# Two transformer layers written out one behind the other in every engine's program, in place of a loop over them

## What is computed

```python
def second_block(x, positions, ...):
    for l in range(DEPTH_2):                      # DEPTH_2 = 2
        mix = token_mixers(x, positions, lam_init, w_in[l], ...)   # four kinds of attention, gated
        x = layer_norm(DN_ALPHA * x + mix, ln1_g[l], ln1_b[l])
        ffn = grouped_moe(x, w_router, router_bias, moe_w1[l], moe_w3[l], moe_w2[l])  # 32 experts
        x = layer_norm(DN_ALPHA * x + ffn, ln2_g[l], ln2_b[l])
    return x
```

## Time and profile before

| | us |
|---|---|
| median of 3 runs (2465.21 to 2465.91) | 2465.53 |
| span of the profiled execution | 2463.8 |
| straight part, up to the layers | about 1055 |
| first pass of the loop, L2751 at 1055.20 to L2751 at 1756.89 | 701.69 |
| second pass, from L2751 at 1756.89 to the end at 2463.8 | 706.9 |

### The profile page before, as it was taken

How to read it: one execution, slowest core, us unless ns; L and a number is a source line. 1 busy time by engine, 2 the same in 40 slices (tenths; PEclk the granted TensorE clock), 3 DMA queues, 4 the chain that set the end, 5 groups by cost and what they waited for, 6 DMA issues and landing times.

```text
span 2463.8 us, 25868 instructions
## 1 busy us (share of the span) xinstructions
PE 2283.6 (93%) x10168; PEld 1569.8 (64%) x10168; DVE 831.3 (34%) x1478; ACT 490.2 (20%) x904; POOL 37.1 (2%) x82
## 2 busy tenths in 40 slices
PE   6999999999988899999999799999799998799997
PEld 3677778756866599768887443334478885533333
DVE  3332332544632365522225411122313144411213
ACT  2111222331312144412221111000102220200101
POOL 0000000100000000000000000000000000000000
PEclk8999999999997999999999899999899999899999
DMA  9555431311310345453212178877533121578792
GB/s 373 213 205 205 171 126 57 117 69 69 137 69 1 137 165 195 151 204 137 103 69 86 45 311 343 336 304 310 202 141 132 69 82 51 209 306 337 323 385 94
DMA packets 49273, 433.46 MB, mean 176 GB/s; under 512 B 6656, under 2 KB 7936, under 8 KB 16000
## 3 DMA queue, kind: packets, MB, share of 16 engines
q1 hardware_dynamic: 45296, 423.35, 44.1%
q10 hardware_dynamic: 3856, 8.42, 1.0%
HBM read 430.71 MB, written 1.05 MB: 175 GB/s over the span
## 4 chain that ended last, share of the span: by engine, by line
issue 57%; PE 39%; DVE 2%; ACT 1%; DMA 1%; POOL 1%; DVEq 0%; POOLq 0%; SPq 0%; ACTq 0%
PE bank L2428 15%; PE bank L2421 5%; PE bank L3062 5%; PE bank L3064 2%; PE bank L3115 2%; PE bank L2365 1%; PE bank L3117 1%; PE bank L2572 1%; PE bank L2530 1%; DMA ring<-in_early 1%; PE bank L3130 1%; PE bank L3026 1%; PE bank L2542 1%; PE bank L2552 1%; PE bank L2377 0%
## 5 line engine op out<-in xcount | busy, mean ns | idle before, releaser
L2421 PE MATMUL bank<-HT,ring 128*128 128x256 f32 (+1 forms) x1984 | 466.6, 395 | 8.1 <-issue 5.9
L2421 PEld LDWEIGHTS bank<-HT,ring 128*128 128x128 f32 x1984 | 375.1, 191 | 91.7 <-issue 45.2
L2428 PE MATMUL bank<-HT_HI,W_HI 128*128 128x512 f32 (+1 forms) x704 | 239.3, 340 | 8.3 <-DVE ring_lo L1564 4.1
L2428 PE MATMUL bank<-HT_HI,ring_lo 128*128 128x512 f32 (+1 forms) x704 | 240.1, 341 | 0.0
L2428 PE MATMUL bank<-HT_LO,W_HI 128*128 128x512 f32 (+1 forms) x704 | 238.1, 338 | 0.0
L3062 PE MATMUL bank<-ring,TOKENS 128*128 128x512 f32 x416 | 190.2, 600 | 3.7 <-issue 3.7
L1012 ACT ACTIVATE W_HI<-ring 128x2048 fp32r<-128x2048 f32 x66 | 126.4, 1915 | 294.6 <-PE bank L2428 228.4
L1564 DVE TENSOR_TENSOR ring_lo<-ring,W_HI 128x2048 fp32r<-128x2048 f32 x66 | 151.0, 2288 | 52.9 <-ACT W_HI L1012 52.8
L2324 DVE SCALAR_TENSOR_TENSOR tmp<-th,bank 128x256 f32<-128x256 f32 x50 | 21.1, 421 | 413.7 <-ACT th L1356 413.7
L2428 PEld LDWEIGHTS bank<-HT_HI,W_HI 128*128 128x128 f32 x704 | 133.3, 189 | 36.2 <-issue 17.1
L2428 PEld LDWEIGHTS bank<-HT_HI,ring_lo 128*128 128x128 f32 x704 | 134.6, 191 | 14.6
(11 more groups left out here) (473 smaller groups left out, 2794.8 us busy)
## 6 DMA issues: line engine op xcount, KB each, us to landing
ring<-in_early SPq DMA_DIRECT2D x64, 2048.0 KB, 8.4
ring<-in_l_moe_in SPq DMA_DIRECT2D x38, 2048.0 KB, 12.3
ring<-in_l_dense SPq DMA_DIRECT2D x30, 2048.0 KB, 7.8
ring<-in_l_moe_out SPq DMA_DIRECT2D x12, 2048.0 KB, 11.6
slot<-in_l_moe_in SPq DMA_DIRECT2D x10, 2048.0 KB, 8.5
HT<-in_l_moe_in SPq DMA_DIRECT2D x8, 2048.0 KB, 10.6
slot_xg<-in_l_moe_in SPq DMA_DIRECT2D x8, 2048.0 KB, 10.9
ring<-in_l_moe_out SPq DMA_DIRECT2D x14, 1024.0 KB, 11.3
```

Of the source, the lines that this page charges most:

```text
L2421: last = mm(out, w[:, k0 + k, c0:c0 + P], rhs(k), start=k == 0, stop=k == kn - 1)
L2428: last = mm(out, a, b, start=start and n == 0, stop=stop and n == 2)
```

## The change

In all five programs `with <engine>.Fori(0, LAYERS) as L:` becomes `for L in range(LAYERS):`, a loop of the language in which the program is written. The body is written out twice, once with `L = 0` and once with `L = 1`; every value made from `L` is a constant; and there is no counter and no branch back. The order of the work on every engine stays the same, and so do its matmuls, transfers and semaphores.

```diff
@@ block.sync @@
-            with sp.Fori(0, LAYERS) as L:
+            for L in range(LAYERS):
                 def free_slot(u):
                     sp.wait_ge(slot_free[u % 4], L * LAYER_TURNS + layer_turn(u))
@@ block.scalar @@
-            with se.Fori(0, LAYERS) as L:
+            for L in range(LAYERS):
 
                 se.wait_ge(layer_start, L + 1)
@@ block.gpsimd @@
-            with po.Fori(0, LAYERS) as L:
+            for L in range(LAYERS):
                 po.wait_ge(c_squares_ready, L + 1)
@@ block.vector @@
-            with ve.Fori(0, LAYERS) as L:
+            for L in range(LAYERS):
                 ve.drain().then_inc(layer_start, 1)
@@ block.tensor @@
-            with pe.Fori(0, LAYERS) as L:
+            for L in range(LAYERS):
                 def take(job):
                     return acquire(pe, at(L, job))
```

## The result

| | median (range), us | ratio to the kernel before, 95% interval |
|---|---|---|
| before | 2465.72 (2465.21 to 2467.15) | |
| after | 2452.51 (2445.63 to 2453.65) | 0.9938 [0.9924, 0.9953] |

So the change saves 13.2 us, 0.6%. The profiled execution took 2452.81 us with a span of 2451.0, 12.8 less than the earlier trace rows. First the page, the span and the busy time of each engine.

What follows compares the result with a forecast made beforehand. The prediction took PE as the bound, busy 2283.6 of 2463.8 us. Branch 4.0, registers 8.0, DVE and ACT 0.3 and clock 2.4 sum to 14.7, giving span 2449.1 and 2450.8 timed, range 2444.5 to 2459.5.

Steps and rivals of the forecast that it cites:

- Part 1: Between the layers on PE: without the taken branch and three steps around it, the second L2751 starts 4.0 us earlier.
- Part 2: In PE's short issue gaps: 91 exposed register steps of 0.09 us go, taken as 8.0 us, bounds 0 and 14.4.
- The list of lines: PE's short gaps: L3094, L2888, L3130 fall to 0.11 or 0.15 us, mostly leaving the issue rows; L3062 keeps its 0.2.
- DVE and ACT: Their adds matter only where PE waits, in the router and at layer end: 0.3 us for both layers, bounds 0 and 1.
- Part 3: Second L2751: with less idle time ahead, PE's half-speed clock there mostly goes, gaining 2.4 us, bounds 0 and 2.7.
- case E: The branch goes, but the low clock stays or moves to other matmuls: 2453.2, up to 2455.5; inside the forecast's 0.72.
- plus or minus 2 us, taken as nothing: Other low-clock stretches, at layer norms and router, may fall on more or fewer matmuls; counted as zero in the sum.
- The first layer: The first pass, which has no branch in it, gets shorter by about 4 us, separating Part 1 from Part 2.
- A: Rival: only the branch counts, as the adds hide in PE's drains; 2459.1 us, chance 0.11.
- D: Rival: waits are still worked out or a barrier comes in, so nothing changes; 2465.5 us, chance 0.04.
- C: Rival: fetching written-out code stalls PE's sequencer, 3.76 us a stall; 2469.6 with five, 2534 at worst; chance 0.04.
- B: Rival: all steps in PE's gaps go (14.4 us), and DVE's and ACT's too, 22.1 us together; 2443.4 us, chance 0.09.

Runs made afterwards that it cites:

- e1b: Kernel before with both layers written out on all engines, but the layer number kept in a register, so register instructions stay and no branch is taken back; 2455.48 us, 0.9970.
- e2: Kernel before with the two layers written out in PE's program alone, the other four engines keeping their loops; 2449.05 us, 0.9938.
- e5: Kernel after with PE's two waits at L2920 named in the other order, ACT's late copy first and the free bank second; 2452.25 us, 0.9953.
- e3: Kernel after with PE's loop kept, so only SP, ACT, POOL and DVE are written out; 2469.62 us, 1.0018 against the kernel before.
- e10: Kernel after with e7's edits, the wait order also swapped on ACT and DVE, and PE's next-weights wait moved ahead of the releasing drain; 2447.15 us, 0.9928.
- a1: Kernel after run again unchanged; 2451.29 us, 0.9948.
- e6: Kernel after with PE's waits in the experts moved ahead of the drain; 2446.49 us, 0.9936.
- e7: Kernel after with the edits of both e5 and e6; 2448.65 us, 0.9942.
- e1: Kernel before with the body written out twice, each copy in a one-pass loop on every engine; register adds vanished, leaving nearly the kernel after; 2451.91 us, 0.9950.
- e9: Kernel before with the loops on all five engines told to fetch their head ahead of the branch back; 2462.23 us, 0.9990.
- e8: Kernel after with a two-pass loop over one drain put into PE's program ahead of the second layer; 2452.23 us, 0.9949.
- e4: Kernel after with PE waiting at the head of the second layer for DVE's signal that it has begun that layer; 2459.24 us, 0.9978.

## Why the prediction was right

The forecast was 2450.8 us, and 2452.5 was measured (2451.3 when the same program was run again). Its 14.7 us stand against 12.8 in the profiled execution. The mechanism of parts 1 and 2 is shown; that the sum came out so near is in part luck, as the parts below tell.

**Part 1, the branch: 4.0 predicted, 4.05 measured, shown.** The branch goes, L2751 starts 4.02 us nearer to the transposes, and e1b alone has 3.84 of it. DVE's and ACT's branches cost nothing as argued: e2, which keeps them, has the whole gain. What was late next is as it was named, the last copies to `HT`, only that it was DVE's copy (L2156) and not ACT's.

**Part 2, the registers: 8.0 predicted, 7.6 measured, but as a sum of two terms, one of which was missing.** The list of lines was right: L3094, L2888 and L3130 dropped out of the issue rows, the pair of the earlier trace rows went to 0.11, and L3062 stayed. The price was too low. The 86 places where a step went gave 10.1 us, 0.117 each, and 0.138 at L2888, where one pair of gaps had given 0.09. Against that stand 2.5 us that the prediction did not have, 1.3 of them at L2920 and 0.7 at the one L2421 a layer that follows DVE's copy to `HT` (L2040), for which no experiment was made. It had set the places where a wait needs an EVENT_SEMAPHORE at no change, and had not asked which wait ends up on it. Where it is the late one, as at L2920, the matmul comes later than before. e5 shows PE's share of L2920, e3 and e10 ACT's. Both errors were about 2 us and took each other away, which is luck.

**DVE and ACT: 0.3 predicted for both layers.** DVE gained 0.3 in each layer at L3013, ACT's order lost 0.3 in each at L2920: nothing is left of it.

**Part 3, the clock: 2.4 predicted, 2.6 measured, and partly luck.** The step said that the idle time ahead of L2751 makes the clock low there and that its end brings the clock back. In the kernel before that is what the windows show, the clock fell a second time in the branch's idle time; and in the traces of after, a1, e2, e5, e6 and e7 it was back in time (11.4 us). In those of e1, e1b and e10, with an idle time of 1.4 to 1.8 us just like theirs, the same matmuls took 13.2 to 14.4. The idle time of 4.7 to 4.9 us ahead of the transposes is enough in some executions, which the prediction named as the case E and gave too little weight: 3 of the 9 traces with an idle time below 2 us went that way, and so did e9, with 2.26 us (14.29). e8, with 2.62 us, had the clock fall inside L2751 (13.11). Over the whole execution the low clock cost 47.8 us before and 45.3 after (half of 95.5 and 90.5), so a gain of 2.5, but a1 would have shown 10. The "plus or minus 2 us, taken as nothing" for the other stretches was too small: equal programs differ by 6.8 us of span, nearly all of it clock, and nearly all in the straight part.

**The first layer: 4 us shorter predicted, 2.7 measured.** 5.0 + 0.3 - 1.1 for steps and router would be 4.1; the clock at L2999 and L3026 took 1.1 of it back, by the chance just named.

**The rivals.** A is refuted by the 2.7 us inside the first layer, by e1b, which has the branch's share without the registers', and by e4, which keeps the registers' share with the branch's idle time back. D is refuted by the rows of L438: no add is left. C, fetch stalls in code written out, did not come: no idle time by issue in a layer is over 0.5 us, and PE's program of 10168 matmuls ran straight. B did not come either, but about as much as its 14.4 us was there to be had, once the waits were moved ahead of the drains: e10 has 7.6 + 6.7 = 14.3, though not all of it from B's gaps, as it has ACT's and DVE's order too. The issue rows of the first layer, the small ones included, sum to 19.2 us before, 13.9 after and 8.0 in e10, so more than half of that idle time was sequencer steps on an empty engine.

## What to carry to other kernels

On PE here a sequencer's step cost nothing while the engine had work queued, and about 0.1 us each time it stood behind a drain or a late wait. So count the steps in the short "issue" gaps, then ask of each whether it can run ahead of the drain, and put the wait that comes last on the working instruction itself. The hardware loop cost its branch once a pass (3.8 us on PE for a body this long), and the registers in every exposed gap (7.6 us in two layers), so a loop of few long passes is a candidate for writing out. And where the clock wanders, compare traces place by place, over the part that differs: a few us of span say nothing alone.

## What the runs showed of the hardware

- A taken compare-and-branch on PE: 3762 and 3726 ns across a layer's code, 407 with a hint, 232 to a head a few instructions back (e8); 76 to 88 when not taken. The 108 ns that the Trainium skill gives ("Advanced Engine Details and Errata", Control Flow Timing) lies between the last two and holds for neither. On DVE and ACT the branch's own record is short (68 and 59 ns at most), and DVE's next copy came 2.20 us behind its last work.
- An add of 32 ns in front of a matmul on an empty PE delays it by 0.09 to 0.14 us, and a matmul one step behind a late EVENT_SEMAPHORE comes 0.06 us and, with the same on the engine that it waits for, 0.12 us later (L2920: 0.25 before, 0.31 in e5, 0.37 after).
- The same program, run twice, had spans of 2451.0 and 2444.2 us; with the low clock's share taken off, 2405.7 and 2406.7. Taking off half of PE's busy time at 0.50 fits the matmuls at the head of the second layer: 11.8 to 15.0 us in the fourteen traces, 11.8 to 12.0 with it taken off.
